# Feed-forward as 2x2 block products, seven for eight, with weight sums made by accumulating transfers

## What is computed

```
def swiglu_ffn(x, g, w_gu, w_down):
    h = rmsnorm(x, g) @ w_gu              # 1024 -> 2 x 2816
    a, b = jnp.split(h, 2, axis=-1)
    return (jax.nn.silu(a) * b) @ w_down  # 2816 -> 1024

for layer in range(2):
    x = x + mixer(x)                      # its last step: @ w_out or @ b_wo
    x = x + swiglu_ffn(x, ffn_norm[layer], w_gate_up[layer], w_down[layer])
```

## Time and profile before

| | |
|---|---|
| runs | 1864.62, 1866.26, 1868.22 us |
| profiled execution: span; its own time | 1864.6; 1864.62 us |
| TensorE matmul busy | 1815.1 us, 97% |
| TensorE weight loads | 1692.6 us, 91% |
| VectorE, ScalarE, GpSimd busy | 913.6, 694.5, 582.0 us |
| granted clock of TensorE | 0.993 of full speed |
| layer 0: gate and up; down | 383 to 664 us; 664 to 806 us |
| layer 1: gate and up; down | 1430 to 1713 us; 1713 to 1857 us |

### The profile page before, as it was taken

How to read it: one execution, slowest core, us unless ns; L and a number is a source line. 1 busy time by engine, 2 the same in 40 slices (tenths; PEclk the granted TensorE clock), 3 DMA queues, 4 the chain that set the end, 5 groups by cost and what they waited for, 6 DMA issues and landing times. The chain is left out here.

```text
span 1864.6 us, 41136 instructions
## 1 busy us (share of the span) xinstructions
PE 1815.1 (97%) x17185; PEld 1692.6 (91%) x17185; DVE 913.6 (49%) x1392; ACT 694.5 (37%) x1097; POOL 582.0 (31%) x298
## 2 busy tenths in 40 slices
PE   8999998999999999999998999999989999999998
PEld 7999997999999999999997677777779999999998
DVE  4757766345555521145653466655543555554000
ACT  5365455431221222245632555555544212222111
POOL 3333221243333343333531011221113333333332
PEclk9999999999999999999999999999999999999999
DMA  5333341222322232242356999999963222223222
GB/s 126 89 97 82 83 111 55 79 80 80 90 81 80 83 93 83 76 142 72 114 178 211 396 386 386 381 360 363 361 217 91 80 80 85 85 80 97 79 78 82
DMA packets 289101, 273.75 MB, mean 147 GB/s; under 512 B 19602, under 2 KB 250099, under 8 KB 288404
## 3 DMA queue, kind: packets, MB, share of 16 engines
q1 hardware_dynamic: 286980, 268.62, 44.1%
q10 hardware_dynamic: 1792, 1.44, 0.3%
q0 software_dynamic: 144, 1.05, 0.2%
HBM read 254.64 MB, written 16.43 MB: 145 GB/s over the span
## 5 line engine op out<-in xcount | busy, mean ns | idle before, releaser
L2020 POOL TENSOR_TENSOR a_wl<-a_wraw,a_wh 128x1024 fp32r<-128x1024 f32 (+2 forms) x91 | 233.5, 2566 | 401.1 <-ACT a_wh L1944 401.0
L2020 POOL TENSOR_TENSOR b_wl<-b_wraw,b_wh 128x1024 fp32r<-128x1024 f32 (+1 forms) x66 | 172.7, 2616 | 298.3 <-ACT b_wh L1944 298.3
L1901 PE MATMUL ps<-xh,a_wh 128*128 128x288 f32 x1104 | 238.4, 298 | 0.0
L1901 PE MATMUL ps<-xh,a_wl 128*128 128x288 f32 x1104 | 236.9, 296 | 0.0
L1901 PE MATMUL ps<-xl,a_wh 128*128 128x288 f32 x1104 | 236.8, 296 | 0.0
L1944 ACT ACTIVATE a_wh<-a_wraw 128x1024 fp32r<-128x1024 f32 (+2 forms) x91 | 100.6, 1106 | 335.5 <-PE ps L1901 315.4
L1944 ACT ACTIVATE b_wh<-b_wraw 128x1024 fp32r<-128x1024 f32 (+1 forms) x66 | 75.0, 1136 | 318.5 <-PE ps L1901 318.5
L2037 DVE TENSOR_TENSOR xT<-xT,ps 128x576 f32<-128x576 f32 x32 | 24.1, 754 | 320.8 <-PE ps L1901 320.8
L1901 PEld LDWEIGHTS ps<-xh,a_wh 128*128 128x128 f32 x1104 | 177.0, 187 | 1.1 <-issue 0.2
L1901 PEld LDWEIGHTS ps<-xh,a_wl 128*128 128x128 f32 x1104 | 177.2, 187 | 0.6
L1901 PEld LDWEIGHTS ps<-xl,a_wh 128*128 128x128 f32 x1104 | 177.2, 187 | 0.6
(11 more groups left out here) (352 smaller groups left out, 3880.6 us busy)
## 6 DMA issues: line engine op xcount, KB each, us to landing
a_wraw<-in_w_gate_up SPq DMA_DIRECT2D x44, 512.0 KB, 3.9
b_wraw<-in_w_gate_up SPq DMA_DIRECT2D x44, 512.0 KB, 3.8
xT<-in_cache_k SPq DMA_DIRECT2D x40, 512.0 KB, 6.4
xT<-in_cache_v SPq DMA_DIRECT2D x40, 512.0 KB, 6.9
a_wraw<-in_a_w_in SPq DMA_DIRECT2D x32, 512.0 KB, 4.2
f_h_plain<-in_cache_k SPq DMA_DIRECT2D x30, 512.0 KB, 6.1
xl_plain<-in_cache_v SPq DMA_DIRECT2D x30, 512.0 KB, 6.8
f_h_plain<-in_cache_v SPq DMA_DIRECT2D x30, 512.0 KB, 6.6
```

The lines of the kernel that those rows point to most:

```text
L1901: mm = pe.matmul(ps[0:width(n), bank(n) + a, 0:HALF], wt[:, base(n) + t, 0:width(n)], ap[:, first + t, a * HALF:(a + 1) * HALF], start=kin ...
L2020: pool.tensor_tensor(part(wl, n), part(wraw, n), part(wh, n).bitcast(F32), ALU.subtract).then_inc(e["low"], 1)
```

## The change

The feed-forward's products are made as products of 2x2 blocks. The weights of a unit are four blocks (two column tiles by even and odd row tiles), the data are four blocks (even and odd row tiles by two token halves), and by the Winograd form of Strassen's scheme seven products of sums of blocks take the place of eight products of blocks. Three things follow in the code.

Units: a "g" unit now holds the gate and the up tile together, and a "d" unit two output tiles. A product is 4 row pairs x 3 = 12 matmuls of 288 columns in a "g" unit and 6 or 9 in a "d" unit (2 or 3 row pairs), so a layer's feed-forward is 22 x 84 + 4 x (42 + 3 x 63) = 2772 matmuls. The hidden tiles are cut into four chunks (4, 6, 6 and 6 tiles), and each chunk's four "d" units stand behind it.

Weights: SyncE issues seven transfers per unit instead of one or two. Four sums of weight blocks are needed (S1, S2, S3, S4). GpSimd issues three accumulating transfers from SBUF to SBUF for them, in a chain: S1 and S3 together (128x1024), then S2 (128x512), which waits for the first to land, then S4, which waits for the second. Each of the seven operands is rounded by ScalarE into one of five slots; the low parts are subtracted by VectorE (products 0, 2, 4, 6) and GpSimd (products 1, 3, 5).

Data: the block sums of the activations are made by VectorE (`cross`), rounded by ScalarE (`round_combinations`) and their low parts made by VectorE (`low_combinations`). Products leave PSUM singly: ScalarE copies the first three of a "g" unit (`snapshot`), and VectorE combines the others (`evict`).

```diff
+A22, A11, S1, S3, A12, S2, S4 = range(7)
+def fast_products():
+    return ((A11, 0, 0), (S1, 1, 2), (S2, 4, 0), (A12, 2, 1), (S3, 5, 0), (S4, 3, 2), (A22, 6, 0))
...
-    CHUNKS = 2
-    UNITS = [("o", f) for f in range(KD)] + [(g, i) for i in range(KF) for g in "gu"] + [
-        ("d" if c < CHUNKS - 1 else "D", f) for f in range(KD) for c in range(CHUNKS)]
+    chunks = [(0, 4), (4, 10), (10, 16), (16, KF)]
...
+    POOLED = (1, 3, 5)
+    SLOTS, AHEAD = 5, 3
...
+                def fetch(n):
...
+                        wait_low(sp, S * (m - 1))
...
+                    for dst, a, x in ((A11, 0, 0), (A22, 1, 1), (S1, 1, 0), (S3, 1, 0)):
+                        sp.dma_start(operand(m, dst), block(a, x)).then_inc(fetched[m % 2], 16)
+                    for dst, a, x in ((S2, 0, 0), (A12, 0, 1), (S4, 0, 1)):
+                        sp.dma_start(operand(m, dst), block(a, x)).then_inc(later[m % 2], 16)
...
+                def product(n, pos):
+                    s = S * m + pos
+                    banks_ready(n, pos)
+                    if pos in POOLED:
+                        pe.wait_ge(e["poollow"], m * len(POOLED) + POOLED.index(pos) + 1)
+                    else:
+                        wait_low(pe, s + 1)
+                    high, low = (slots[i][s % SLOTS] for i in range(2))
+                    for t, q in enumerate(pairs):
...
+                        for i, (wt, part) in enumerate(((high, 0), (high, 1), (low, 0))):
+                            mm = pe.matmul(place(m, pos), wt[:, at], combination(tile, part, b), ...
...
+                def round_part(s):
+                    m, pos = divmod(s, S)
+                    if s >= SLOTS:
+                        act.wait_ge(e["multiplied"], s - SLOTS + 1)
...
+                    if which in sums:
+                        act.wait_ge(sums[which][m % 2], m // 2 * 16 + 16)
+                    act.activation(slot(s, 0), operand(m, which), ACT.Copy).then_inc(e["parthigh"], 1)
...
+                def snapshot(n, pos):
+                    act.wait_ge(e["multiplied"], S * m + pos + 1)
+                    act.activation(dst, place(m, pos), ACT.Copy).then_inc(e["snapped"], 1)
...
+                    elif n in fast:
+                        for pos in range(S):
+                            if kind(n) == "g" and pos < 3:
+                                snapshot(n, pos)
+                            round_part(S * (n - KD) + pos + AHEAD)
+                            if pos == (0 if own(n) else 2) and parted(n) is not None:
+                                round_combinations(KD + parted(n))
...
+                            if pos == 6:
+                                if kind(n) == "g":
+                                    silu(UNITS[n][1])
...
+                def add_operands(n):
+                    pool.wait_ge(fetched[i], 4 * done)
+                    pool.dma_start(operand(m, S1, 2), operand(m, A22, 2), accum_op=ALU.add).then_inc(sums[S1][i], 16)
+                    pool.wait_ge(later[i], 3 * done)
+                    pool.wait_ge(sums[S1][i], done)
+                    pool.dma_start(operand(m, S2), operand(m, S1), accum_op=ALU.add).then_inc(sums[S2][i], 16)
+                    pool.wait_ge(sums[S2][i], done)
+                    pool.dma_start(operand(m, S4), operand(m, S2), accum_op=ALU.add).then_inc(sums[S4][i], 16)
...
+                    if n in fast:
+                        for pos in POOLED:
+                            s = S * (n - KD) + pos
+                            pool.wait_ge(e["parthigh"], s + 1)
+                            pool.tensor_tensor(slot(s, 1), operand(n - KD, PRODUCTS[pos][0]), slot(s, 0).bitcast(F32), ALU.subtract
+                                               ).then_inc(e["poollow"], 1)
+                        add_operands(n + 1)
+                        continue
...
+                def low_part(s):
+                    dve.wait_ge(e["parthigh"], s + 1)
+                    dve.tensor_tensor(slot(s, 1), operand(m, PRODUCTS[pos][0]), slot(s, 0).bitcast(F32), ALU.subtract).then_inc(e["partlow"], 1)
```

More of the change, by code:

```diff
@@ new lines, in combination, with combinations, source, groups @@
+        def combination(t, part, b):
+            most, more, q = blocks_of(t, part)
+            return most[:, b, q, :] if b < 4 else more[:, b - 4, q, :]
+        def combinations(t, part, group):
+            most, more, q = blocks_of(t, part)
+            return (most[:, 0:2, q, :], more[:, 0:3, q, :], most[:, 2:4, q, :])[group]
+        def source(group):
+            return (even[:, 0:3:2, :], odd[:, 2:5, :], odd[:, 0:2, :])[group]
+        def groups(t):
+            return (1, 2) if t % 2 else (0,)
@@ L1824, in part, with operand @@
         def part(tile, n):
-            return tile[:, base(n):base(n) + depth(n), 0:width(n)]
+            first = plain(n) % 2 * KD
+            return tile[:, first:first + KD, 0:width(n)]
         def out(n):
             return ps[0:width(n), bank(n):bank(n) + 2, 0:HALF]
+        def operand(m, which, count=1):
+            w = len(pairs_of(KD + m)) * P
+            tile = (4 * which if which < A12 else {A12: 16, S2: 38, S4: 60}[which]) if m % 2 == 0 else 22 + 4 * which + (6 if which >= A12 else 0)
+            r, at = divmod(tile, KF)
+            ap = rings[r][:, at * P:(at + 4 * count) * P].rearrange("p (x n) -> p x n", x=count)[:, :, 0:w]
+            return ap if count > 1 else ap[:, 0, :].rearrange("p (q n) -> p q n", n=P)
@@ L1886, in unit @@
-                    if kind(n) != "D" and m >= 2:
-                        pe.wait_ge(e["freed"], m - 1)
-                    pe.wait_ge(e["low"], n + 1)
-                    high, low, first = {"o": (sh, sl, 0), "d": (k.fh, k.fl, 0), "D": (k.fh, k.fl, KW)}.get(kind(n), (k.xh, k.xl, 0))
-                    if kind(n) in "dD":
-                        pe.wait_ge(e["flow"], KW if kind(n) == "d" else KF)
-                    for t in range(begun if n == 0 else 0, depth(n)):
+                    if plain(n) >= 2:
+                        pe.wait_ge(e["freed"], plain(n) - 1)
@@ L1893, in unit @@
+                    if TAIL <= n < TAIL + 2:
+                        pe.wait_ge(e["taken"], take[F - 2 + n - TAIL, 6] + 1)
+                    pe.wait_ge(e["low"], plain(n) + 1)
+                    high, low = (sh, sl) if kind(n) == "o" else (k.xh, k.xl)
+                    first = plain(n) % 2 * KD
+                    for t in range(begun if n == 0 else 0, KD):
                         if split and n == 0:
                             pe.wait_ge(split.rest, t + 1)
-                        if n == KD or n == TAIL:
-                            pe.wait_ge(e["xlow"], t + 1 + (KD if n == TAIL else 0))
+                        if n == TAIL:
+                            pe.wait_ge(e["xlow"], t + 1)
@@ L1918, in _ @@
                 for n in range(N):
-                    unit(n)
-                    if not heads and kind(n) == "D" and UNITS[n][1] > 0:
-                        turn_out(UNITS[n][1] - 1)
+                    if n not in fast:
+                        unit(n)
+                    else:
+                        for pos in range(S):
+                            product(n, pos)
+                            if n == KD and pos == 3:
+                                mean(0)
+                            if not heads and n > TAIL - ROWS and pos in (1, 3):
+                                turn_out(2 * (UNITS[n][2] - 1) + (1 if pos == 3 else 0))
@@ new lines, in evict @@
+                def evict(n, pos):
+                    m, i = n - KD, UNITS[n][1]
+                    before = {3: 0, 4: 1, 5: 2}
+                    if kind(n) == "d":
+                        j = UNITS[n][2]
+                        tile, half = ((0, 0), (1, 1), (0, 1), (0, 0), (1, 1), (0, 1), (1, 0))[pos]
+                        dst = k.xT[:, 2 * j + tile, half * HALF:(half + 1) * HALF]
+                        if pos in before:
+                            dve.wait_ge(e["taken"], take[m, before[pos]] + 1)
+                    else:
+                        tile = 1
+                        src = {3: kept[:, i % 2, 0, :], 4: up[:, i % 2, :], 5: kept[:, i % 2, 1, :]}[pos]
+                        dst = {3: gate[:, 0, :], 4: up[:, i % 2, :], 5: gate[:, 1, :]}[pos]
+                        dve.wait_ge(e["snapped"], snap[m, before[pos]] + 1)
+                    dve.wait_ge(e["multiplied"], S * m + pos + 1)
+                    if kind(n) == "d":
+                        src = dst
+                    elif pos in (3, 5) and i > 0:
+                        dve.wait_ge(e["scaled"], i)
+                    dve.tensor_tensor(dst, src, place(m, pos), ALU.add if tile else ALU.subtract).then_inc(e["taken"], 1)
```

443 lines of the change are left out of this document (319 added, 124 removed).

## The result

| | before | after |
|---|---|---|
| median | 1866.55 us (1864.62 to 1868.22, 4 runs) | 2552.58 us (2550.72 to 2553.97, 4 runs) |
| ratio | | 1.3669, 95% interval 1.365 to 1.3689 |
| matmuls | 17185 in the trace | 16393 in the trace |
| TensorE busy | 97% | 75% |
| mean granted clock over the span | 0.993 | 0.872 |

The change costs 686 us. The direction and the kind of cause were forecast, the size was not: 2552.6 lies above the whole range of 1830 to 2300.

What follows compares the result with a forecast made beforehand. The prediction took GpSimd's chain of accumulating transfers to bound the changed kernel: 1864.6 us + 196 for the chain + 10 for starts and ends = 2071, as a median 2072. Range 1830 to 2300.

Steps and rivals of the forecast that it cites:

- what would bound: Feed-forward: the chain of sums binds at about full clock, TensorE's longest waits before product 1 being for GpSimd's low part.
- what comes: the chain of accumulating transfers: GpSimd's in-order queue: waited-for sums lengthen "g" units to 15.5 us and "d" units to 11.6 or 10.3, +196 us.
- X: "g" unit loop: landing of S1 with S3, landing of S2 and issue of S4, taken as 8.7 us.
- the high end: Chain of sums with 1.1 us more per step for GpSimd's slow issue: 9.8 us in a "g" unit, +280 us.
- starts them a unit ahead, so they are hidden: SyncE's seven transfers per unit, 2.6 us of issue, were taken as hidden.
- whose round: GpSimd in "d" units: three landings in a row, then rounding and low part of product 5; 11.6 or 10.3 us.
- the loop's constant: "g" unit, product 2 to product 2: snapshot, rounding, two low parts and products 1 and 2, together 6.8 us.
- rival B: TensorE's stalls also cost clock: 1.6 us per stall in 76 units, +120, 2190 to 2280 us; chance 0.29 with the full-DMA rival.
- rival C: DMA engines fill up in the feed-forward, landings grow towards 6.9 us, time past 2250; chance 0.29 with the clock rival.
- the forecast's case: Feed-forward bound by the chain of sums at about full clock, 1870 to 2180 us; chance 0.50.
- rival A: Feed-forward: sums land fast and the gain of fewer matmuls comes, from 1760 us to nothing, given as 1810; chance 0.21.
- the 10 us for the starts: Start and end of each layer's feed-forward, first loads, sums and low parts in sequence: 5 us per layer, +10.

Runs made afterwards that it cites:

- Experiment 1: The changed kernel with all accumulating transfers left out, operands multiplied as loaded: 1909.6 us.
- Experiments 2: The changed kernel with weights loaded only for the first two units of a layer's feed-forward, sums kept: 2316.4 us.
- 6: The changed kernel with SyncE starting a unit's loads only when S2 of the unit before has landed: 2362.9 us.
- 15: The changed kernel with copies in place of accumulating transfers and weights loaded only for a layer's first two units: 2043.5 us, ratio 1.0942 to the kernel before.
- Experiment 4: The changed kernel with unused matmuls behind product 0, 45 in "g" and 22 in most "d" units, to keep TensorE awake: 2528.0 us.
- experiment 14: The changed kernel without sums, GpSimd's and VectorE's low parts of weights filled with zeros, weights loaded only for a layer's first two units: 1856.5 us.
- 13: The changed kernel without sums, low parts of weights filled with zeros on both GpSimd and VectorE, loads kept: 1857.8 us, ratio 0.9947 to the kernel before.
- 10: The changed kernel without sums, VectorE making a weight's low part ahead of block sums, scaling and gating: 1902.5 us, ratio 1.0189 to the kernel before.

## Why the prediction was wrong

**Right: what would bound.** GpSimd's waits for its own sums inside a loop from product 2 to product 2, and TensorE's longest wait the one before product 1, for L2288. Experiment 1 shows it (643 of 686 us). Right too that nothing of the matmuls' number failed (792 gone) and that VectorE stays below 85%.

**Wrong: the step "what comes: the chain of accumulating transfers", its term X.** 8.7 us were taken, 13.5 are measured; the high end was 9.8. By parts: S1 with S3 4.2 forecast, 5.1 measured; S2 3.3 against 7.8; S4's issue, the rest of X, 1.2 against 0.57 (the high end's basis, GpSimd's issue of 1.50 us for the gather, is 0.86 for these transfers). So S2 alone adds 4.5 us to a total error of 4.8. Two costs make it, and neither was in the sum. The loads of the unit after next were booked as "starts them a unit ahead, so they are hidden": hidden from TensorE they are, but they lie on the DMA engines just when S2 does, since a low part of VectorE (604.62 to 605.31 us) lets them go at 605.38, 3 us behind S1 and 2 ahead of S2, and much the same in every "g" unit that follows another (2.6 to 3.1 us behind S1, the second of the layer apart). Experiments 2 and 6 show that cost, 236 and 190 us. And the bounds for a sum were taken from plain transfers with GpSimd's slow issue on top, none of which adds; experiments 2 and 15 show 4.5 and 3.3 us for what is 2.9 and 2.3 as a copy. By an estimate from the Trainium skill ("DMA: Bandwidth & Descriptors", Anatomy of one DMA), about 2 us plus the bytes over 436 GB/s, 512 KB take 3.2 us. That is near the copy's 2.9, and 1.3 short of the sum's 4.5 even without loads.

The same term is short in the "d" units, whose round was rightly described: 16.8 us in the mean for 11.6, and 13.5 for 10.3. Without loads (experiment 2) those of three row pairs still take 12.9 to 14.1 in the second and third chunk. Of the 240 us a layer that the forecast missed, 22 x 6.5 = 143 are in the "g" units and 12 x 5.2 + 4 x 3.2, about 75, in the "d" units; the rest lies in the starts and the changes from one kind to the other.

**Wrong: the loop's constant.** 6.8 us forecast, 9.5 measured (23.0 - 13.5). Of the 2.7 more, 2.4 are products 1 and 2 (5.6 for 3.2) and 0.4 the low part of product 1 (1.64 for 1.28). TensorE isn't idle once in these two products, but its granted clock is 0.50 from 617.5 to 622 us, so the 2.4 are almost all clock. Experiment 4 gives only 1.4 of them back, since at the higher clock TensorE waits for VectorE's low part of product 2. That is rival B in place, but small: its price of 1.6 us per stall was about right. The number of stalls that pay it was not. The prediction charged all 76 units, though by its own account no product lies in the round of a "d" unit, and there experiment 4 gained nothing.

**Wrong: the test for rival C.** Its decision point was a DMA share above 0.9 in the stage. The stage shows 0.55 to 0.58, and yet the engines are at 0.91 to 1.01 for 10 us, and S2 is under way in most of them. A mean over the stage can't decide on a chain that meets a burst. By the other half of its test, landings above 6 us, C is what happened (6.8). Rather than a case of its own it was the size of X in the forecast's case, and its price "past 2250" was on the right side.

**Wrong: rival A's ceiling.** It was given 1810 us and a chance of 0.21. Without any cost of the sums the kernel stands at 1909.6, without GpSimd's subtractions at 1867.9, without the weights' subtractions on either engine at 1857.8. The prediction counted VectorE's work (8.7 to 12.5 us of 11.2) but as a sum over the unit. What the traces show are waits for it before single products, of 0.63 us in the row shown for experiment 14. Of the 97 us from 1857.8 to 1761 (1866.6 - 105.8) the runs exclude the loads (experiment 14) and the subtractions' length (13). The cause of the rest stays open; the order of the elementwise work is likely, but the one experiment on it (10) gained 7 us.

**Short: the 10 us for the starts.** In after the first product starts at 392.5 us in layer 0, where the kernel before starts its at 383.2. From the end of this feed-forward to the first product of layer 1 it is 632.5 us (1150.5 to 1783.0) for 623.5 (806.8 to 1430.3). That is 18 us for both, before any wait for the first chain.

## What to carry to other kernels

A transfer that is waited for must be priced with what is under way at that moment: look at the DMA share in slices of the wait's own length (5 us here), not of the stage, and ask what event starts the loads. A chain of waited-for transfers on an in-order engine cost less here by being spread between that engine's other work (2203.8 us for 2552.6, with the same transfers) than by being shortened in place (2412.4, with one transfer more). And before a saving on the bounding engine is booked, run the kernel with the new cost left out: here that upper bound was already slower than before.

## What the hardware showed that was not expected

- An accumulating transfer within SBUF lands later than a copy of the same size: 512 KB 4.5 against 2.9 us, 256 KB 3.3 against 2.3, both without loads beside them. Its issue on GpSimd takes 0.86 against 0.54 us, and for 70.27 MB it needs 37072 packets for 20688, and 407 against 188 us of all 16 DMA engines. From 256 to 512 KB a sum takes 1.2 us more, a copy 0.6.
- Beside seven loads a 256 KB sum takes 6.8 us in the median and 7.8 in the turn shown, at a DMA share of 1.01 and 251 GB/s.
- Behind a stall of 8.5 us the granted clock was 0.50 (1.2 GHz), from 617.5 to 622 us, and two products took 5.6 us for 3.2. Kept busy in the stall, TensorE got 0.945 in the mean, and the kernel gained 25 us of 2553: where the stall itself is the bound, its clock is a small part.
- GpSimd's subtractions beside VectorE's cost a kernel 42 us more than fills with zeros (1909.6 and 1867.9), nearly all by way of VectorE: TensorE's waits for VectorE's low parts fell by 43 us.
